# HGRN heads: the next head's projections in ten portions between the tile steps, operands of two heads side by side, diagonal blocks placed by one product

## The chip, the core and the metric

The kernel runs on one core of a Trainium2 chip. The core has five engines with queues of their own: TensorE (PE; its weight loads are shown apart as PEld), VectorE (DVE), ScalarE (ACT), GpSimd (POOL) and SyncE (SP, which issues DMAs). Each works through its queue in order; they wait for one another through semaphores. The metric is the device time of one execution in microseconds; lower is better.

## What is computed

Two transformer blocks of 256 tokens, one after the other, in float32. The change touches one mixer of the second block, HGRN2: four heads with key and value width 128, over 256 latent and 256 context tokens, forwards and backwards, with a decay per key column:

```python
def forget_gate(f_raw, lb):
    z = f_raw.astype(jnp.float32)
    log_f = jnp.logaddexp(jnp.log(lb), jnp.log1p(-lb) + jax.nn.log_sigmoid(z))
    k = (1.0 - lb) * jax.nn.sigmoid(-z)
    return k, log_f

def step(S, inp):                       # one chunk of 32 tokens
    qc, kc, gc, vc = inp
    b = jnp.cumsum(gc, axis=2)
    diff = b[:, :, :, None, :] - b[:, :, None, :, :]
    decay = jnp.exp(jnp.where(tri, diff, -jnp.inf))
    scores = jnp.einsum("bhtd,bhtsd,bhsd->bhts", qc, decay, kc)
    o = jnp.einsum("bhts,bhsv->bhtv", scores, vc) + jnp.einsum("bhtd,bhdv->bhtv", qc * jnp.exp(b), S)
    ...

def readout(o, g):
    return (rms_norm(o, out_norm_w).reshape(B_, n, B_V_W) * jax.nn.silu(g)).astype(g.dtype)
```

Queries are `silu(h @ w)` times a scale; here `lb` is zero, so the key is `sigmoid(-z)` and the log decay is `log_sigmoid(z)`. Each head needs five projections of the same 512 token columns: queries (Q), forward and backward forget logits (K0, K1), values (V) and gates (G), each by a 1024 x 128 weight.

## The kernel before

`hgrn_phase` (L2249) holds one program per engine. Matrix products of float32 are made from three products of rounded parts: a weight is split into `w_hi` (a rounding copy, ACT, L2485) and `w_lo` (the rest, by subtraction); the tokens `h_hi`, `h_lo` lie ready. So one projection is 8 x 3 = 24 matmuls of 512 columns (`part`, L2354), and values with gates together are 4 x 24 matmuls of 256 columns (`values_and_gates`, L2363).

A head's attention goes over eight tile steps, two directions by four tiles of 128 tokens. In step u TensorE makes the sums of the log decays over nine ranges (`sums`, L2389, six matmuls into banks 0 to 2), ACT takes their exponential into `e` (L2534, double buffered), VectorE multiplies seven of them with the queries into `qd` (L2671) and one into `qs` (L2673), GpSimd does the same with the keys, `kd` and `ke` (L2611, L2613). TensorE makes the scores of five short ranges and the diagonal in 32 x 32 blocks, and of two long ranges in end blocks (`scores`, L2405, L2408, L2411, banks 3 and 4). VectorE masks the blocks (`pm`, L2656) and adds the six up, once for each quarter of the partitions, right into the diagonal of the probabilities `pr` (L2662); ACT copies the end blocks beside them (L2526). TensorE multiplies `pr` with the values into bank 7 (L2418), one step later. After the eight tiles come the products between tiles (`cross_scores` L2437 into banks 5 and 6, `px` L2545, `cross_values` L2444), the norm of the output (ACT L2551 and L2554, VectorE L2689 and L2693) and its transposes (L2451), copied to `y_T` (L2575).

The next head's five projections run after the tile steps of this one, between those last products: `part(i+1, 0)` after step 8, 1 and 2 about the cross scores, values and gates last, into banks 0 to 4, which the tile steps use also. `w_hi` and `w_lo` have two slots; GpSimd subtracts for parts 0 and 1 (L2601), VectorE for 2 to 4 (L2625). ACT takes the queries' silu and the keys' sigmoid straight from PSUM (L2489, L2494), keeps `|z|` (L2495), and makes the log decay by exp and ln (L2500, L2503) and VectorE's L2642; TensorE turns it to token-major (L2373), ACT and VectorE split it (L2515, L2631). All five weights of a head are loaded by SP in one go when the split of the former head is done. The first three heads run in a hardware loop (`heads`, with `eng.Fori`), the fourth is written out.

The order on each engine is written out by hand: what stands first in the text goes first.

## Time and profile before

| | us |
|---|---|
| median of 3 runs | 2715.73 (2714.08 to 2720.18) |
| the profiled execution, device time | 2714.51 |
| its span, first to last instruction | 2712.7 |
| PE busy | 2422.6 (89%) |
| PEld busy | 2084.3 (77%) |
| DVE busy | 1358.3 (50%) |
| ACT busy | 1135.7 (42%) |
| POOL busy | 212.1 (8%) |
| mean granted TensorE clock | 0.923 of full speed |

The rows come from the profiled execution. Busy time is the time in which an engine's instructions run; matmuls are pipelined, so a busy PE can still be below its peak. The granted clock is the share of 2.4 GHz that TensorE was given (1.0 is 2.4 GHz, 0.5 is 1.2 GHz; numbers between are a mixture over a stretch). An idle time ends with a releaser: who gave the last semaphore, or "issue" where nothing in the profile shows what was waited for. The HGRN phase is some 13% of the span; all else is the same code before and after.

### The profile page before, as it was taken

To read this page: it belongs to the slowest core of one execution; us is meant where nothing else is said; L and a number is where in the kernel's file an instruction comes from. 1 tells how busy PE (TensorE), PEld (TensorE's weight loads), DVE (VectorE), ACT (ScalarE), POOL (GpSimd) and SP (SyncE) were. 2 spreads that over 40 slices of the span, in tenths; PEclk is the share of its full clock that TensorE was granted. 3 is DMA by queue.
4 is the path that set the end of the run, shared out by engine and by line. 5 is a ranking of instruction groups with operands and counts; after the bars stand their busy time and mean duration, and the time that the engine had idled before them with its cause. 6 is when DMAs were issued, how large, how long until landed. Compare 5 with 4: busy or idle time off the path is not lost. (4 is left out here: it accounts for less than half of the span.)

```text
span 2712.7 us, 42379 instructions
## 1 busy us (share of the span) xinstructions
PE 2422.6 (89%) x16488; PEld 2084.3 (77%) x16488; DVE 1358.3 (50%) x2193; ACT 1135.7 (42%) x1993; POOL 212.1 (8%) x185
## 2 busy tenths in 40 slices
PE   7998999998998998998768887678999989996998
PEld 6887978887887977887446776566888778875997
DVE  5443246445444236444445556646555554435665
ACT  3443254334434234443264444334333444444554
POOL 1000001001000001000003324300000000001000
PEclk9999899998999979999897888788999987997999
DMA  7876124875786323885121120023333362202663
GB/s 226 258 244 187 34 67 138 249 249 154 239 246 207 69 63 93 240 254 158 51 61 40 40 70 0 1 62 109 115 116 115 103 171 63 71 32 88 199 186 93
DMA packets 395134, 350.09 MB, mean 129 GB/s; under 512 B 25364, under 2 KB 358408, under 8 KB 394504
## 3 DMA queue, kind: packets, MB, share of 16 engines
q1 hardware_dynamic: 384932, 297.81, 38.1%
q10 hardware_dynamic: 10084, 50.66, 5.2%
q8 instruction: 81, 1.33, 0.2%
q14 instruction: 37, 0.30, 0.0%
HBM read 347.38 MB, written 1.05 MB: 128 GB/s over the span
## 5 line engine op out<-in xcount | busy, mean ns | idle before, releaser
L523 PE MATMUL ps<-x_hi,gu_hi 128*128 128x256 f32 x1680 | 478.4, 285 | 0.0
L523 PE MATMUL ps<-x_lo,gu_hi 128*128 128x256 f32 x1680 | 475.4, 283 | 0.0
L523 PE MATMUL ps<-x_hi,gu_lo 128*128 128x256 f32 x1680 | 475.4, 283 | 0.0
L523 PEld LDWEIGHTS ps<-x_hi,gu_hi 128*128 128x128 f32 x1680 | 321.9, 192 | 22.6 <-DVE gu_lo L668 17.5
L523 PEld LDWEIGHTS ps<-x_lo,gu_hi 128*128 128x128 f32 x1680 | 322.2, 192 | 2.6
L523 PEld LDWEIGHTS ps<-x_hi,gu_lo 128*128 128x128 f32 x1680 | 322.2, 192 | 0.0
L668 DVE TENSOR_TENSOR gu_lo<-w_gu,gu_hi 128x1024 fp32r<-128x1024 f32 x220 | 266.9, 1249 | 87.0 <-ACT gu_hi L599 87.0
L599 ACT ACTIVATE gu_hi<-w_gu 128x1024 fp32r<-128x1024 f32 x220 | 221.9, 1051 | 44.9 <-issue 30.0
L610 ACT ACTIVATE silu<-ps 128x256 f32<-128x256 f32 x88 | 33.8, 384 | 418.7 <-PE ps L523 404.8
L694 DVE SCALAR_TENSOR_TENSOR hid<-silu,ps 128x256 f32<-128x256 f32 x88 | 37.0, 421 | 316.9 <-ACT silu L610 316.8
L549 PE MATMUL ps<-dn_hi,h_hi 128*128 128x512 f32 x440 | 173.9, 395 | 6.4 <-DVE h_lo L703 6.3
L549 PE MATMUL ps<-dn_lo,h_hi 128*128 128x512 f32 x440 | 173.1, 393 | 0.0
L549 PE MATMUL ps<-dn_hi,h_lo 128*128 128x512 f32 x440 | 171.7, 390 | 0.0
L676 DVE TENSOR_TENSOR dn_lo<-w_dn,dn_hi 128x1024 fp32r<-128x1024 f32 x110 | 133.8, 1220 | 10.7 <-ACT dn_hi L603 10.7
L819 PE MATMUL ps<-both_x_hi,gu_hi 128*128 128x512 f32 x336 | 130.7, 389 | 0.0
L819 PE MATMUL ps<-both_x_lo,gu_hi 128*128 128x512 f32 x336 | 130.7, 389 | 0.0
L819 PE MATMUL ps<-both_x_hi,gu_lo 128*128 128x512 f32 x336 | 130.7, 389 | 0.0
L603 ACT ACTIVATE dn_hi<-w_dn 128x1024 fp32r<-128x1024 f32 x110 | 115.1, 1051 | 17.3 <-PE ps L549 17.3
L549 PEld LDWEIGHTS ps<-dn_hi,h_hi 128*128 128x128 f32 x440 | 83.3, 189 | 22.0 <-issue 7.4
L977 DVE SCALAR_TENSOR_TENSOR conv<-ps,par,conv 128x510 f32<-128x510 f32 x44 | 30.9, 745 | 134.4 <-ACT conv L914 134.4
L549 PEld LDWEIGHTS ps<-dn_hi,h_lo 128*128 128x128 f32 x440 | 83.1, 189 | 18.2
L549 PEld LDWEIGHTS ps<-dn_lo,h_hi 128*128 128x128 f32 x440 | 83.4, 190 | 13.4
(419 smaller groups left out, 5354.0 us busy)
## 6 DMA issues: line engine op xcount, KB each, us to landing
w_gu<-in_ffn_w_up SPq DMA_DIRECT2D x178, 512.0 KB, 6.1
w_dn<-in_ffn_w_down SPq DMA_DIRECT2D x134, 512.0 KB, 3.7
w_mod<-in_w_mod ACTq DMA_DIRECT2D x64, 768.0 KB, 6.4
w_gu<-in_ffn_w_gate SPq DMA_DIRECT2D x90, 512.0 KB, 5.1
odd_w<-in_odd_w_qkv SPq DMA_DIRECT2D x24, 512.0 KB, 5.2
w_gu<-in_ffn_w_down SPq DMA_DIRECT2D x11, 1024.0 KB, 4.9
hgrn_w<-in_even_w_in SPq DMA_DIRECT2D x20, 512.0 KB, 7.0
w_in_q<-in_w_in SPq DMA_DIRECT2D x2, 3072.0 KB, 10.9
```

The lines of the kernel that those rows point to most:

```text
L523: last = pe.matmul(gu(n)[:, a, :], wt[n][:, a, f, :], x[:, f, :], start=(f == 0 and p == 0), stop=(f == FT - 1 and p == 2), skip_group_che ...
L549: last = pe.matmul(k.ps[:, 2 * tt + c, :], h[n][:, tt * P:(tt + 1) * P], wt[n][:, c * BANK:(c + 1) * BANK], start=(first and p == 0), stop ...
L599: act.activation(gu_hi[n][:, a, :, :], wgu[n][:, a, :, :], ACT.Copy).then_inc(s["w_hi"], 1)
L603: act.activation(dn_hi[n][:, :], wdn[n][:, :], ACT.Copy).then_inc(s["w_hi"], 1)
L610: act.activation(sil[n][:, :], gu(n)[:, 0, :], ACT.Silu).then_inc(s["act_done"], 1)
L668: last = dve.tensor_tensor(gu_lo[n][:, a, :, :], wgu[n][:, a, :, :], gu_hi[n][:, a, :, :].bitcast(F32), ALU.subtract)
L676: dve.tensor_tensor(dn_lo[n][:, :], wdn[n][:, :], dn_hi[n][:, :].bitcast(F32), ALU.subtract).then_inc(s["dn_split"], 1)
L694: dve.scalar_tensor_tensor(hid[n][:, :], sil[n][:, :], 0.5, gu(n)[:, 1, :], ALU.mult, ALU.mult).then_inc(s["h_full"], 1)
L819: last = pe.matmul(gu(n, a), wt[n][:, a, f, :], x[:, f, :], start=(f == 0 and p == 0), stop=(f == FT - 1 and p == 2))
L977: dve.scalar_tensor_tensor(cv[n][:, a, :, 1:S], streams(n, a)[:, :, 0:S - 1], conv.tap(0, t, a), cv[n][:, a, :, 1:S], ALU.mult, ALU.add).t ...
```

## The change

Everything in it lies in `hgrn_buffers`, `hgrn_load` (one raw weight, in the order K0, K1, Q, G, V) and `hgrn_phase`, with one more constant (`c_blk`, ones in the four 32 x 32 blocks of the diagonal).

- The projections of head i+1 are cut into ten portions (`slot`): two each for K0, K1, Q, and four token tiles of gates and values. Portion u stands in tile step u, between sums and scores; portions 9 and 10 stand behind the last step. From the second head on all go into bank 6, one projection after the other, and ACT copies each out as it is (`keep_keys`, `keep_queries`, `keep_values`). For the first head there are five banks.
- `q`, `kk` and `vg` (values and gates) have two halves, one for each of two heads in turn. The silus come later, from SBUF, together (`silus`); the key is now exp(-softplus(z)), with VectorE's `max(z,0)+ln(...)` ahead of ACT's exp, so that no sigmoid is used.
- Raw weights come one projection at a time through two slots (`w_in`), the split weights through three; all `w_lo` are made by VectorE.
- `kd` and `ke` move from GpSimd to VectorE. VectorE adds up all 128 partitions at once into a narrow `prc`; GpSimd spreads it over the four diagonal blocks with one product with `blk` (`place`), which also writes the zeros around them, and takes the column `tot` (`total`).
- End blocks have two banks (4, 5), and the cross scores use banks 4 and 5 now. `px` has one buffer; the cross products of the two directions follow each other. The value product of a tile comes three steps later, the norm and the output of a head in the next head's first steps.
- The head loop is written out for all four heads on every engine.

```diff
+WRING = 3
+RAWRING = 2
+HGRN_PARTS = (1, 2, 0, 4, 3)
...
+    K0, K1, Q, G, V = range(5)
+    VG01, VG23 = 3, 4
+    SLOTS = [(K0, 0), (K0, 1), (K1, 0), (K1, 1), (Q, 0), (Q, 1), (VG01, 0), (VG01, 1), (VG23, 0), (VG23, 1)]
+    LAST = BH - 1
...
+            END_PS = [k.ps[:, 4 + n, 0:3 * SUB] for n in range(2)]
+            X_PS = flat[:, 4 * BANK:4 * BANK + 6 * P]
...
+            def proj_bank(h, c):
+                return k.ps[:, (4, 5, 6, 3, 7)[c] if h == 0 else 6, :]
...
+                for p in range(RAWRING, 5 * BH):
+                    sp.wait_ge(s["w_lo"], p - RAWRING + 1)
+                    dst, src = hgrn_load(m, w, p)
+                    sp.dma_start(dst, src).then_inc(w_in[p % RAWRING], 16)
...
+                def slot(h, n):
+                    c, half = SLOTS[n]
+                    bank = proj_bank(h, c)
+                    pe.wait_ge(s["w_lo"], 5 * h + (c if c < VG01 else V) + 1)
+                    if half == 0 and h:
+                        pe.wait_ge(s["proj_used"], 5 * h + c)
+                    if c < VG01:
+                        for f in range(4 * half, 4 * half + 4):
+                            for p, (wt, x) in enumerate(SPLITS):
+                                last = pe.matmul(bank, wt[:, f, (5 * h + c) % WRING, :], x[:, f, :], start=(f == 0 and p == 0),
+                                                 stop=(f == FT - 1 and p == 2))
                     else:
+                        tt = 2 * (c - VG01) + half
                         for f in range(FT):
                             for p, (wt, x) in enumerate(SPLITS):
+                                last = pe.matmul(bank[:, half * 2 * P:(half + 1) * 2 * P].rearrange("p (a n) -> p a n", a=2),
+                                                 x[:, f, tt * P:(tt + 1) * P], wt[:, f, gate_and_value(h)[2], :],
+                                                 start=(f == 0 and p == 0), stop=(f == FT - 1 and p == 2), skip_group_check=True)
+                    if half == 1:
+                        last.then_inc(s["proj_done"], 1)
...
+                    if d == 0:
+                        pe.wait_ge(s["ends_ready"], unit(i, NU - 1))
...
+                for n in range(8):
+                    slot(0, n)
+                turn_decays(0)
+                for n in range(8, 10):
+                    slot(0, n)
+                sums(0, 0)
+                for i in range(BH):
+                    more = i < LAST
+                    for u in range(NU):
+                        if u:
+                            sums(i, u)
+                        if more:
+                            slot(i + 1, u)
+                        if u == 2 and i:
+                            turn_out(i - 1)
+                        if u >= 1:
+                            scores(i, u - 1)
+                        if u >= 3:
+                            values(i, u - 3)
+                    if more:
+                        turn_decays(i + 1)
+                        slot(i + 1, 8)
+                    scores(i, NU - 1)
+                    values(i, NU - 3)
                     cross_scores(i, 0)
                     if more:
+                        slot(i + 1, 9)
+                    values(i, NU - 2)
+                    cross_values(i, 0)
                     cross_scores(i, 1)
+                    values(i, NU - 1)
                     if more:
+                        sums(i + 1, 0)
+                    cross_values(i, 1)
+                turn_out(LAST)
...
+                def split(h, j):
+                    p = 5 * h + j
+                    if p >= RAWRING:
+                        act.wait_ge(w_in[p % RAWRING], 16 * (p // RAWRING))
+                    if p >= WRING:
+                        before = p - WRING
+                        act.wait_ge(s["proj_done"], before // 5 * 5 + (before % 5 if before % 5 < G else VG23) + 1)
+                    act.activation(w_hi[:, :, p % WRING, :], wh[:, p % RAWRING, :, :], ACT.Copy).then_inc(s["w_hi"], 1)
...
+                def keep_keys(h, d):
+                    act.wait_ge(s["proj_done"], 5 * h + d + 1)
+                    if h:
+                        act.wait_ge(s["g_turned"], 2 * h)
+                    act.activation(ab[:, d, :], proj_bank(h, d), ACT.Abs).then_inc(s["abs_ready"], 1)
+                    act.activation(z[:, d, :], proj_bank(h, d), ACT.Copy).then_inc(s["proj_used"], 1)
...
+                def decay_tile(i, u):
+                    act.wait_ge(s["cum_done"], unit(i, u))
+                    n = i * NU + u - 2
+                    if n >= 0:
+                        act.wait_ge(s["side_done"], n + 1)
+                        act.wait_ge(s["tot_ready"], n + 1)
...
+                def score_ends(i, u):
+                    d = UNITS[u][0]
+                    act.wait_ge(s["sc_done"], unit(i, u))
+                    act.wait_ge(s["placed"], unit(i, u))
...
+                for i in range(BH):
+                    more = i < LAST
+                    for u in range(NU):
+                        decay_tile(i, u)
+                        if u >= 2:
+                            score_ends(i, u - 2)
+                        if u == 0:
+                            if more:
+                                split(i + 1, K1)
+                            if i:
+                                norm(i - 1)
+                        if u == 1 and more:
+                            keep_keys(i + 1, 0)
+                        if u == 2:
+                            if more:
+                                split(i + 1, Q)
+                            if i:
+                                keep_output(i - 1)
+                        if u == 3 and more:
+                            split(i + 1, G)
+                            keep_keys(i + 1, 1)
+                        if u == 4 and more:
+                            split(i + 1, V)
+                            soft_exp(i + 1)
+                        if u == 5 and more:
+                            keep_queries(i + 1)
+                        if u == 6 and more:
+                            soft_ln(i + 1)
+                        if u == 7 and more:
+                            keep_values(i + 1, VG01)
+                            keys(i + 1)
+                    if more:
+                        decays_hi(i + 1)
+                    score_ends(i, NU - 2)
+                    score_ends(i, NU - 1)
+                    keep_cross(i, 0)
+                    if more:
+                        keep_values(i + 1, VG23)
+                        silus(i + 1)
+                    keep_cross(i, 1)
+                    if i + 2 <= LAST:
+                        split(i + 2, K0)
...
+                def place(i, u):
+                    pool.wait_ge(s["p_ready"], unit(i, u))
+                    n = i * NU + u - 2
+                    if n >= 0:
+                        pool.wait_ge(s["pv_done"], n + 1)
+                    pool.tensor_tensor(pr[:, u % 2, :].rearrange("p (b n) -> p b n", n=SUB), m.blk[:, :].rearrange("p (b n) -> p b n", n=SUB),
+                                       prc[:, u % 2, :].unsqueeze(1).broadcast_to([P, P // SUB, SUB]), ALU.mult).then_inc(s["placed"], 1)
...
+                def decays(h):
+                    for d in range(2):
+                        dve.wait_ge(s["ln_step"], 2 * h + d + 1)
+                        dve.wait_ge(s["proj_used"], 5 * h + d + 1)
+                        dve.scalar_tensor_tensor(keys_of(h, d), z[:, d, :], 0.0, ab[:, d, :], ALU.max, ALU.add).then_inc(s["k_pre"], 1)
+                        dve.scalar_tensor_tensor(z[:, d, :], z[:, d, :], 0.0, ab[:, d, :], ALU.min, ALU.subtract).then_inc(s["g_ready"], 1)
...
+                def products(i, u):
+                    d, tt = UNITS[u]
+                    if u == 0:
+                        dve.wait_ge(s["k_ready"], 2 * i + 2)
+                        dve.wait_ge(s["q_ready"], i + 1)
+                        if i:
+                            dve.wait_ge(s["x_done"], 2 * i)
+                    dve.wait_ge(s["e_ready"], unit(i, u))
+                    n = i * NU + u - 2
+                    if n >= 0:
+                        dve.wait_ge(s["sc_done"], n + 1)
+                    key, qry = kk[:, i % 2, d, tt, :], q[:, i % 2, tt, :]
+                    times = lambda to, a, n, b: dve.tensor_tensor(to, a, b.unsqueeze(1).broadcast_to([P, n, P]), ALU.mult)
+                    times(kd[:, u % 2, :, :], e[:, u % 2, 1:N8, :], NLV, key)
+                    times(qd[:, u % 2, :, :], e[:, u % 2, 1:N8, :], NLV, qry).then_inc(s["qk_ready"], 1)
+                    dve.tensor_tensor(ke[:, u, :], e[:, u % 2, 0, :], key, ALU.mult)
+                    dve.tensor_tensor(qs[:, u, :], e[:, u % 2, N8, :], qry, ALU.mult).then_inc(s["side_done"], 1)
...
+                def probs(i, u):
+                    dve.wait_ge(s["sc_done"], unit(i, u))
+                    if u >= 2:
+                        dve.wait_ge(s["p_ready"], unit(i, u - 2))
+                    dve.tensor_tensor(pm[:, u % 2, :], SC_PS, lvl[:, UNITS[u][0], :], ALU.mult).then_inc(s["masked"], 1)
+                    dve.wait_ge(s["masked"], unit(i, u))
+                    if u >= 2:
+                        dve.wait_ge(s["placed"], unit(i, u - 2))
+                    dve.reduce_sum(prc[:, u % 2, :], pm[:, u % 2, :].rearrange("p (n t) -> p t n", t=SUB), AX.X).then_inc(s["p_ready"], 1)
...
+                for i in range(BH):
+                    more = i < LAST
+                    for u in range(NU):
+                        products(i, u)
+                        if u >= 1:
+                            probs(i, u - 1)
+                        if u == 0 and more:
+                            split(i + 1, K1)
+                        if u == 1 and i:
+                            norm(i - 1)
+                        if u == 2 and more:
+                            split(i + 1, Q)
+                        if u == 3 and more:
+                            split(i + 1, G)
+                        if u == 4 and more:
+                            split(i + 1, V)
+                        if u == 6 and more:
+                            decays(i + 1)
                     cross_operands(i)
                     if more:
+                        decays_lo(i + 1)
+                    probs(i, NU - 1)
                     if more:
+                        queries_and_gates(i + 1)
+                    if i + 2 <= LAST:
+                        split(i + 2, K0)
+                norm(LAST)
```

The order on VectorE in one tile step with a weight split in it. Before (`hgrn_tot` is the total decay, `pm` the masked scores):

```order
L2670 COPY hgrn_tot<-hgrn_e 128x1
L2671 TENSOR_TENSOR hgrn_qd<-hgrn_e,hgrn_q 128x896
L2673 TENSOR_TENSOR hgrn_qs<-hgrn_e,hgrn_q 128x128
L2656 TENSOR_TENSOR hgrn_pm<-ps,hgrn_lvl 128x192
L2662 TENSOR_REDUCE hgrn_p<-hgrn_pm 32x32 x4
```

and now:

```order
L2744 TENSOR_TENSOR hgrn_kd<-hgrn_e,hgrn_k 128x896
L2744 TENSOR_TENSOR hgrn_qd<-hgrn_e,hgrn_q 128x896
L2747 TENSOR_TENSOR hgrn_ke<-hgrn_e,hgrn_k 128x128
L2748 TENSOR_TENSOR hgrn_qs<-hgrn_e,hgrn_q 128x128
L2754 TENSOR_TENSOR hgrn_pm<-ps,hgrn_lvl 128x192
L2758 TENSOR_REDUCE hgrn_pc<-hgrn_pm 128x32
L2708 TENSOR_TENSOR hgrn_w_lo<-hgrn_w,hgrn_w_hi 128x8x128
```

The keys' products have come to VectorE, the column copy has gone, one reduction stands where four stood, and a `w_lo` follows in five of eight steps.

TensorE in one tile step, sums, scores, value product. Before:

```order
L2389 MATMUL ps<-hgrn_cum,hgrn_g_hi 128x384
L2389 MATMUL ps<-hgrn_cum,hgrn_g_lo 128x384
...
L2405 MATMUL ps<-hgrn_qd,hgrn_kd 32x32 x20
L2405 MATMUL ps<-hgrn_q,hgrn_k 32x32 x4
L2408 MATMUL ps<-hgrn_qd,hgrn_kd 32x32 x2
L2411 MATMUL ps<-hgrn_qd,hgrn_kd 64x64
L2418 MATMUL ps<-hgrn_v,hgrn_p 128x128
```

and now:

```order
L2427 MATMUL ps<-hgrn_cum,hgrn_g_hi 128x384
L2427 MATMUL ps<-hgrn_cum,hgrn_g_lo 128x384
...
L2396 MATMUL ps<-hgrn_h_hi,hgrn_w_hi 128x512
L2396 MATMUL ps<-hgrn_h_lo,hgrn_w_hi 128x512
L2396 MATMUL ps<-hgrn_h_hi,hgrn_w_lo 128x512
...
L2446 MATMUL ps<-hgrn_qd,hgrn_kd 32x32 x20
L2446 MATMUL ps<-hgrn_q,hgrn_k 32x32 x4
L2449 MATMUL ps<-hgrn_qd,hgrn_kd 32x32 x2
L2452 MATMUL ps<-hgrn_qd,hgrn_kd 64x64
L2463 MATMUL ps<-hgrn_vg,hgrn_p 128x128
```

A portion of twelve matmuls with the next head's weights stands between the sums and the scores of the tile before.

TensorE behind the eighth step of a head, now: scores of tile 7, a value product, cross scores of direction 0, portion 10, a value product, cross values, then direction 1. `px` is the copy of the cross scores.

```order
L2446 MATMUL ps<-hgrn_qd,hgrn_kd 32x32 x20
L2446 MATMUL ps<-hgrn_q,hgrn_k 32x32 x4
L2449 MATMUL ps<-hgrn_qd,hgrn_kd 32x32 x2
L2452 MATMUL ps<-hgrn_qd,hgrn_kd 64x64
L2463 MATMUL ps<-hgrn_vg,hgrn_p 128x128
L2471 MATMUL ps<-hgrn_qs,hgrn_ke 128x128 x2
...
L2471 MATMUL ps<-hgrn_qx,hgrn_ke 128x128
L2402 MATMUL ps<-hgrn_w_hi,hgrn_h_hi 128x256
...
L2463 MATMUL ps<-hgrn_vg,hgrn_p 128x128
L2477 MATMUL ps<-hgrn_vg,hgrn_px 128x128 x6
L2471 MATMUL ps<-hgrn_qs,hgrn_ke 128x128 x2
```

Of the projections only these 24 small matmuls of portion 10 and portion 9 ahead of the scores are left between the heads; before, three parts of 24 matmuls and the 96 of values and gates stood there.

## Rows read from the trace of the kernel before

**Rows 1.** stretches: length, busy us (instructions) of PE, PEld, DVE, ACT, POOL, clock, DMA.

```profile
1461.00:1502.00 41.00, 27.81 (x493) 22.59 (x493) 37.62 (x60) 15.85 (x34) 29.38 (x18) 0.68 0.01 2
1502.00:1543.00 41.00, 39.47 (x239) 34.83 (x240) 11.85 (x23) 23.05 (x38) 2.20 (x1) 0.95 0.26 65
1510.00:1526.00 16.00, 16.00 (x96) 14.10 (x95) 3.00 (x4) 8.19 (x11) 0.00 (x0) 1.00 0.00 0
1705.00:1746.00 41.00, 26.98 (x496) 21.07 (x494) 37.56 (x63) 15.37 (x34) 26.09 (x16) 0.74 0.01 2
```

**Rows 2.** ACT timeline, start and head 1: start us, us, line, [idle before].

```profile
1420.87 2.00 ACT L2485 ACTIVATE hgrn_w_hi<-hgrn_w 128x1024 fp32r<-128x1024 f32 x2 [0.28 <-PEq L204]
...
1462.48 1.13 ACT L2534 ACTIVATE hgrn_e<-ps 128x1152 f32<-128x1152 f32 x1 [1.23 <-PE ps L2389]
```

**Rows 3.** ACT timeline, the fourth (last) head.

```profile
1707.54 1.13 ACT L2534 ACTIVATE hgrn_e<-ps 128x1152 f32<-128x1152 f32 x1 [0.96 <-PE ps L2389]
...
1738.17 1.13 ACT L2534 ACTIVATE hgrn_e<-ps 128x1152 f32<-128x1152 f32 x1 [1.70 <-PE ps L2389]
...
1763.13 0.60 ACT L2575 ACTIVATE y_T<-ps 128x512 f32<-128x512 f32 x1 [2.40 <-PE ps L2451]
```

**Rows 4.** a stretch, L2354 (K and Q projections) alone: PE, PEld, clock.

```profile
1511.60:1516.60 5.00, 5.00 (x24) 4.13 (x22) 1.00 0.00 0
```

**Rows 5.** the same of L2363 (gates and values).

```profile
1450.00:1456.00 6.00, 6.00 (x52) 6.00 (x52) 1.00 1.13 270
```

**Rows 6.** stretches, PE alone: a value product and six sums; one scores.

```profile
1736.50:1738.00 1.50, 1.42 (x8) 1.00 0.00 0
1739.30:1740.50 1.20, 0.94 (x54) 1.00 0.05 14
```

**Rows 7.** stretches of L2437 (cross scores), L2444 (cross values), L2373 (transposes), each alone.

```profile
1509.90:1511.70 1.80, 1.50 (x12) 1.42 (x12) 1.00 0.00 0
...
1523.50:1526.60 3.10, 2.84 (x24) 2.73 (x24) 1.00 0.00 0
...
1539.20:1540.40 1.20, 1.04 (x8) 0.81 (x8) 1.00 0.00 0
```

**Rows 8.** timeline of the first tile step, VectorE beside GpSimd.

```profile
1463.69 2.08 POOL L2611 TENSOR_TENSOR hgrn_kd<-hgrn_e,hgrn_k 128x896 f32<-128x896 f32 x1 [37.01 <-ACT hgrn_e L2534]
1463.71 3.00 DVE L2671 TENSOR_TENSOR hgrn_qd<-hgrn_e,hgrn_q 128x896 f32<-128x896 f32 x1
```

**Rows 9.** instructions on tile hgrn_e: ns min/median/max, first, last start.

```profile
L2534 ACT ACTIVATE hgrn_e<-ps x32: 1131/1131/1132, 1462.5 to 1738.2; 128x1152 f32<-128x1152 f32 x32
...
L2671 DVE TENSOR_TENSOR hgrn_qd<-hgrn_e,hgrn_q x32: 1081/2218/3226, 1463.7 to 1741.3; 128x896 f32<-128x896 f32 x32
L2613 POOL TENSOR_TENSOR hgrn_ke<-hgrn_e,hgrn_k x32: 450/1302/1415, 1465.7 to 1741.4; 128x128 f32<-128x128 f32 x32
L2673 DVE TENSOR_TENSOR hgrn_qs<-hgrn_e,hgrn_q x32: 279/540/2423, 1466.6 to 1742.3; 128x128 f32<-128x128 f32 x32
```

**Rows 10.** groups by form, the phase: xcount, busy us, mean ns, idle.

```profile
L2662 DVE TENSOR_REDUCE hgrn_p<-hgrn_pm 32x32 f32<-32x192 f32 x128 | 61.7, 482 | 2.4
...
L2625 DVE TENSOR_TENSOR hgrn_w_lo<-hgrn_w,hgrn_w_hi 128x1024 fp32r<-128x1024 f32 x12 | 14.7, 1226 | 44.9 <-ACT hgrn_w_hi L2485 44.9
...
L2656 DVE TENSOR_TENSOR hgrn_pm<-ps,hgrn_lvl 128x192 f32<-128x192 f32 x32 | 11.1, 347 | 0.1
...
L2642 DVE SCALAR_TENSOR_TENSOR hgrn_abs<-ps,hgrn_abs 128x512 f32<-128x512 f32 x8 | 5.2, 692 | 13.7 <-ACT hgrn_abs L2503 13.7
...
L2503 ACT ACT_TABLE_LOAD x4 | 5.1, 1283 | 0.1
```

**Rows 11.** tile hgrn_w: loads, issue to landing.

```profile
DMA to landing us min/median/max: 3.8/7.0/10.3
```

**Rows 12.** waits, looped head 2, then unlooped head 4: us, times, longest.

```profile
PEld ps L2405 <- issue: 1.4, 3, 0.5
...
PEld ps L2405 <- issue: 3.6, 3, 2.2
```

461 lines of the change are left out of this document (173 added, 288 removed).

## The prediction, made before the changed kernel was run

> **What bounds the kernel now.** The granted-clock view came first (one core, mean 0.923), then busy time by stretch. The change touches one phase, the HGRN heads, from 1420.9 to 1763.7 us [rows 2, 3]: 342.8 us. Everything else keeps its instructions. The first exponentials of heads 1 and 4 start at 1462.48 and 1707.54 [rows 2, 3], so one head lasts 245.06 / 3 = 81.7 us. It has two halves. In the tile loop (41 us) VectorE is busy 37.6 us, GpSimd 29.4, TensorE 27.8 at a granted clock of 0.68; in the transition (41 us) TensorE is busy 39.5 at 0.95 and VectorE 11.9, GpSimd 2.2 [rows 1]. Each half is bound by one side while the other rests. That is the point to see: the sum of both engines' work is far below the sum of the halves.
>
> Why is VectorE full in the loop? `qd` starts at 1463.71 and takes 3.00 us; `kd` on GpSimd starts 0.02 earlier and takes 2.08; the fastest `qd` takes 1.08 [rows 8, 9]. 2.08 + about 1.0 is 3.0: one engine stands still while the other multiplies. The small products show it too: `ke` 0.45 at best and 1.30 in the median, `qs` 0.28 and 0.54 [rows 9]. The Trainium skill ("SBUF — State Buffer", Who interferes with whom) says that VectorE and GpSimd share a port pair under an exclusive lock, held for a whole instruction; the trace agrees (3.00 for 2.08 plus 1.0).
>
> **The change, part by part.** *Removed from VectorE's path:* waiting for GpSimd's 2.08 us product, and three of four reductions of 0.48 us per tile [rows 8, 10]. *Added:* `kd` and `ke`. A tile step now costs VectorE 2 x 1.08 + 2 x 0.28 + 0.35 + 0.48 = 3.55 us [rows 9, 10]; I take the one 128-partition reduction at the 0.48 of the 32-partition one, because both read 192 elements per partition (bounds: 0.48, and 1.93 for four). GpSimd keeps a one-column copy and one 128x128 product: 0.45 us, or 1.30 with VectorE in its way [rows 9]. That takes up to 0.45 from VectorE. Per head VectorE has 8 x 4.0 = 32, five `w_lo` of 1.23 (two were GpSimd's) = 6.1, four decay steps of 0.69 = 2.8 (two before) [rows 10], and some 6 unchanged: 47 us.
>
> *Moved:* TensorE's projections of the next head. At clock 1.00, 24 matmuls of 512 columns fill 5.00 us and 52 of 256 columns 6.00 [rows 4, 5]: a K or Q portion (12) is 2.5 us, a gate-and-value portion (24) 2.8. One head then is: K0, K1, Q 72 x 0.21 = 15.1; gates and values 96 x 0.115 = 11.0; sums with a value product 8 x 1.42 = 11.4; scores 8 x 0.94 = 7.5 [rows 6]; cross scores 2 x 1.50 = 3.0, cross values 2.8, decay transposes 1.0 [rows 7], output transposes (four of the same) 0.5, the zeroing product about 1.0 (an estimate, two 512-column passes at twice 0.21, rounded up). Sum 53.3. With no gap in the queue the clock should stay up: it was 1.00 in the stretch in which TensorE was busy 16 of 16 us and 0.95 with 39.5 of 41 [rows 1]; I take 0.95, so 56.1.
>
> *New waits.* (1) `cross_scores(0)` now waits for `ends_ready` of tile 7, since its banks 4 and 5 hold the end blocks. Queued on VectorE before it: tile 7's scores end 1.0 after portion 9; mask and reduction 0.9, placing 0.5, ACT's three end copies 0.7; TensorE has one value product of 0.3 meanwhile: 2.1 idle. Behind that wait stand portion 10 and both cross values. (2) At the first step of a head ACT has table load, exponential, a split of 1.05, the previous head's four squares (1.2), table load, root, table load, then the second exponential: 1.28 + 1.13 + 1.05 + 1.2 + 1.28 + 0.3 + 1.28 + 1.13 = 8.7 us [rows 9, 10], while TensorE has cross values 1.4, portion 1, sums, portion 2 and scores, 8.5; sums(2) follow ACT. About 1 us idle. (3) The single projection bank 6: portion 3 waits for ACT to copy K0 out (two copies, 1.1 us); TensorE has scores and sums, 2.1 us, in between. Cost nothing, unless ACT is late. (4) The raw weights come through a ring of two. A load takes 3.8 to 10.3 us [rows 11]; each is wanted two portions or more (10 us) after its slot is free. Nothing; SP's queue holds nothing else but the four output-row loads, which go out in head 3. (5) For small hand-overs I add 2 us a head. 56.1 + 2.1 + 1 + 2 = 61.2: **61 us a head**. In a step TensorE has 5.0 us, VectorE 4.0, or 5.2 with a `w_lo`: near each other, which is why the high end is wide. ACT has some 41 us a head, with six table loads of 1.28.
>
> On those table loads the Trainium skill ("ScalarE: Activation LUTs", What ACT_TABLE_LOAD costs) adds a drain of 1.38 us to each load of 1.28. The trace disagrees: the loads of L2503 stand 1283 ns, 0.1 us idle in front of four of them together [rows 10].
>
> *Start.* `w_lo` of the first part moves from GpSimd to VectorE, the projections run in the order K0, K1, Q, G, V with values last. Q's load can only start when K0's split is done, about 1423.3, lands by 1434 at the worst and is wanted at 1436. TensorE then is through at about 1455, but ACT still copies the last bank, does two silus behind a table load and reloads: first exponential about 1459, 3 us earlier. One us of it is given back in the next head, whose offset is smaller: net 2. *Last head.* No portions to hide; VectorE at 4.0 a tile against (1738.17 - 1707.54) / 7 = 4.38 now [rows 3], but with the previous head's norm inside it: nothing to 3 us. Its tail has cross values and cross scores in turn through one `px` buffer (+1) and one reduction instead of four, twice (-3). Together 2.
>
> **Sum.** 3 x (81.7 - 61) + 2 + 2 = 66 us. The profiled execution took 2714.5 (span 2712.7), 1.2 below the median of 2715.7; 2714.5 - 66 = 2648.5, **2648 us**.
>
> Bounds: at clock 1.00 and with waits of 2.7 only, a head is 56: -81, 2633. If VectorE and the lock set the pace at 6.0 a step, and the transition keeps 22: 70 a head, -39 + 3 for a last head that gains nothing: 2682.
>
> **Rivals.**
> 1. *Partly late ACT or VectorE.* The portions fit, but each step waits about 1.2 us for bank 6 to be copied out or for VectorE behind `w_lo`: 61 + 10 = 71 a head; 2714.5 - 32 - 2 = 2680. For it: 5.2 against 5.0 us in five steps; in-order ACT. Against: averages of 47 and 41 in 61.
> 2. *The clock stays down.* Loops of scores ran at 0.68 and 0.74 [rows 1]. If the mixed stream is granted 0.72, 53.3 becomes 74, with 3 idle 77: 2714.5 - 14 - 2 = 2698. Against: TensorE had a third of that stretch idle, and will not.
> 3. *Slower: the chain closes.* If in each step the next sums wait for everything before them (portion 2.8, sums 1.1, exponential 1.3, products 2.7, scores 0.9, mask and reduction 0.9, placing 0.5 to 1.3, ends 0.7), a step is 11 us and a head 88 + 22 = 110: 2714.5 + 85 = 2800. It decides from a step of (81.7 - 22) / 8 = 7.5 us on. Against: buffers of e, kd, qd, pm and pr are double, end blocks now too, and the value product comes three steps late, so only sums to exponential to sums (2.4) and portion to copy to portion are tight.
> 4. *Unlooped code.* All heads are now straight code. In looped head 2 issue waits before scores are 1.4 us in total, in the straight head 4 3.6, longest 2.2 [rows 12]. At twice 2.2 a head more: 65, 2661. The Trainium skill ("Runtime: NRT & Kernel Launch", Instruction fetch mechanics) says that taken branches stall the fetch and straight code streams; by that rule this rival costs nothing.
> 5. *Table drain.* Were the drain there, three loads near the head's edge would add 4 us a head: 2714.5 - 54 = 2661. The skill's page above gives that rule; the row speaks against it.
> 6. *Nothing gained*: the phase is reordered and late waits eat all. 2714.5.
>
> **Chances.** Forecast 0.68 (own range 2633 to 2664), rival 1 0.14, 2 0.05, 3 0.05, 4 0.03, 5 0.01, 6 0.04. Leaving out 2, 3, 6 and a little of the rest, the range is 2630 to 2685. A measurement tells about 0.2% (5.4 us) from no change: faster 0.91, same 0.03, slower 0.06.
>
> **What would show it.** First exponentials of heads 61 us apart; TensorE busy over 90% and granted 0.95 or more between them; `kd` and `qd` 1.1 us each; the placing product 0.5 to 1.3; one idle gap of about 2 us a head before cross scores. Wrong if the sums wait on ACT in most steps, if the portions wait for bank 6, or if the granted clock in the loop stays near 0.7.

## The result and the profile after

| | before | after |
|---|---|---|
| median, us | 2714.9 (4 runs, 2712.4 to 2720.2) | 2630.7 (4 runs, 2627.9 to 2632.6) |
| ratio, 95% interval | | 0.9687 [0.9668, 0.9705] |
| profiled execution, us | 2714.5 | 2632.3 |
| its span | 2712.7 | 2630.5 |
| mean granted clock | 0.923 | 0.937 |
| PE busy in the span | 2422.6 | 2389.3 |

The kernel became 84 us faster; the forecast was 66. The two profiled executions differ by 82.2, and 81.8 of it lie in the phase: it ends at 1681.9 in place of 1763.7 [rows 3]. ScalarE's timeline after, first exponential of each head and the last copy (it answers [rows 2, 3]):

```profile
1458.75 1.13 ACT L2585 ACTIVATE hgrn_e<-ps 128x1152 f32<-128x1152 f32 x1
...
1515.42 1.13 ACT L2585 ACTIVATE hgrn_e<-ps 128x1152 f32<-128x1152 f32 x1
...
1572.94 1.13 ACT L2585 ACTIVATE hgrn_e<-ps 128x1152 f32<-128x1152 f32 x1
...
1629.53 1.13 ACT L2585 ACTIVATE hgrn_e<-ps 128x1152 f32<-128x1152 f32 x1
...
1681.29 0.60 ACT L2611 ACTIVATE y_T<-ps 128x512 f32<-128x512 f32 x1 [2.37 <-PE ps L2484]
```

The first exponential stands 3.7 us earlier. Three heads take 56.9 us each in place of 81.7, which makes 74.3. The last head with its tail takes 52.4 in place of 56.2, which makes 3.8. Together that is 81.8.

Stretches of after, one head each (columns as [rows 1]); then the tile steps and the edge of the second head apart:

```profile
1458.70:1515.40 56.70, 53.07 (x710) 47.07 (x710) 38.13 (x65) 34.60 (x61) 13.68 (x16) 0.97 0.13 39
1515.40:1572.90 57.50, 55.01 (x726) 48.28 (x726) 39.45 (x70) 38.69 (x73) 12.95 (x16) 1.00 0.16 47
1572.90:1629.50 56.60, 54.59 (x724) 48.03 (x725) 38.21 (x69) 37.78 (x72) 12.95 (x16) 1.00 0.20 67
1629.50:1682.00 52.50, 32.58 (x552) 26.49 (x551) 30.19 (x62) 23.10 (x58) 12.48 (x16) 0.82 0.01 1
...
1515.40:1557.00 41.60, 41.48 (x571) 35.34 (x572) 34.30 (x61) 30.67 (x59) 12.20 (x15) 1.00 0.22 65
1557.00:1573.00 16.00, 13.59 (x158) 13.00 (x157) 5.14 (x10) 8.10 (x16) 0.75 (x2) 1.00 0.00 1
```

The two halves of a head [rows 1] have become one. In the eight tile steps TensorE is busy 41.48 of 41.60 us at the full 2.4 GHz; all its idle time stands in the last 16 us. VectorE has 39 of 57, so TensorE bounds a head. Its waits from 1515 to 1573 us (us, times, longest):

```profile
PE ps L2471 <- ACT hgrn_p L2594: 1.9, 1, 1.9
PE ps L2396 <- DVE hgrn_w_lo L2708: 1.1, 2, 0.5
```

The first is `cross_scores(0)` behind ScalarE's end copies; the second is portion 1 behind a late `w_lo`, 0.5 us for each of the two head edges that touch the window. The first has a price beyond its length. In the first head the same wait of 1.9 us ends at 1503.5, and behind it TensorE falls to its low level (1.2 GHz) for some 3 us while it is fully busy; in the second and third head it does not fall:

```profile
1502.00:1504.00 2.00, 0.51 (x2) 0.54 (x3) 0.10 (x1) 0.60 (x3) 0.45 (x1) 0.78 0.00 0
1504.00:1506.00 2.00, 2.00 (x12) 2.00 (x11) 0.00 (x0) 0.00 (x0) 0.00 (x0) 0.50 0.03 8
1506.00:1508.00 2.00, 2.00 (x16) 2.00 (x16) 0.00 (x0) 0.81 (x1) 0.00 (x0) 0.87 0.00 0
```

That is the 0.97 of the first head. What VectorE and GpSimd do, by tile and by form (it answers [rows 9, 10]):

```profile
L2685 POOL COPY hgrn_tot<-hgrn_e x32: 183/1084/1213, 1459.9 to 1661.5; 128x1 f32<-128x1 f32 x32
L2744 DVE TENSOR_TENSOR hgrn_kd<-hgrn_e,hgrn_k x32: 1079/1092/1349, 1460.0 to 1660.1; 128x896 f32<-128x896 f32 x32
L2744 DVE TENSOR_TENSOR hgrn_qd<-hgrn_e,hgrn_q x32: 1077/1085/1353, 1461.0 to 1661.1; 128x896 f32<-128x896 f32 x32
...
L2758 DVE TENSOR_REDUCE hgrn_pc<-hgrn_pm 128x32 f32<-128x192 f32 x32 | 16.1, 503 | 1.1
...
L2693 POOL TENSOR_TENSOR hgrn_p<-hgrn_blk,hgrn_pc 128x128 f32<-128x128 f32 x32 | 25.9, 810 | 83.4 <-DVE hgrn_pc L2758 80.7 <-PE ps L2463 2.7
...
L2607 ACT ACT_TABLE_LOAD x4 | 5.1, 1283 | 0.1
```

`qd` fell from a median of 2218 ns to 1085. The exclusion between the two engines is still there, but now GpSimd pays: its one-column copy takes 183 ns at best and 1084 in the median, the length of one of VectorE's wide products.

### The profile page after: what moved, and what is told of

It reads as the page before. It is cut to its first block and busy times, and to the rows that moved or that the text cites. A ratio compares the mean times of both kernels' runs of the same rounds, so it can differ in the third digit from the quotient of the medians.

```text
span 2630.5 us, 42098 instructions
## 1 busy us (share of the span) xinstructions
PE 2389.3 (91%) x16488; PEld 2060.9 (78%) x16488; DVE 1317.9 (50%) x2144; ACT 1135.1 (43%) x1996; POOL 140.4 (5%) x177
```

## The experiments

Single executions of one kernel spread over up to 12 us, and the medians of the kernel before, measured anew beside each group of runs, lie between 2712.4 and 2714.9. So the length of the phase (ScalarE's first split to the start of its last `y_T` copy, from the timelines) stands beside the medians. It repeats better: 260.7 and 260.3 in two executions of the changed kernel. A ratio is to the kernel before that was measured beside the run. A head is the time from its first exponential to that of the next head.

| kernel | median us | ratio to before | phase us | heads 1, 2, 3 us |
|---|---|---|---|---|
| before | 2714.9 | | 342.3 | 81.0, 81.3, 82.8 |
| after | 2630.7 | 0.9687 | 260.7 | 56.7, 57.5, 56.6 |
| e1 portions behind | 2683.6 | 0.9883 | 310.2 | 70.7, 75.0, 74.1 |
| e2 keys on GpSimd | 2636.1 | 0.9711 | 262.2 | 56.1, 57.3, 57.9 |
| e3 two products | 2618.4 | 0.9651 | 246.8 | 51.2, 54.9, 51.5 |
| e4 VectorE loaded | 2641.1 | 0.9729 | 270.1 | 58.8, 60.5, 58.1 |
| e5 fill | 2629.0 | 0.9688 | 255.9 | 54.0, 56.3, 55.3 |
| e6 both | 2626.1 | 0.9675 | 253.2 | 53.1, 55.4, 55.4 |
| e7 four openings | 2624.3 | 0.9673 | 250.5 | 52.3, 54.6, 54.6 |
| e8 before, filled | 2722.2 | 1.0030 | 351.7 | 86.5, 89.0, 82.7 |
| e9 before, straight | 2712.7 | 1.0002 | 341.8 | 80.8, 82.9, 80.8 |
| e10 filled, straight | 2714.4 | 0.9999 | 340.8 | 81.5, 81.7, 81.8 |
| e11 before, keys moved | 2713.2 | 1.0002 | 341.5 | 82.3, 82.1, 81.9 |
| e12 one opening | 2622.0 | 0.9675 | 250.6 | 52.3, 54.6, 54.6 |
| e13 portions only | 2640.0 | 0.9725 | 267.9 | 58.0, 59.3, 59.8 |
| e14 before, placing | 2777.0 | 1.0230 | 406.7 | 98.6, 98.8, 98.7 |
| e15 after again | 2630.6 | 0.9696 | 260.3 | 56.9, 57.6, 56.6 |
| e16 one opening again | 2621.4 | 0.9660 | 250.6 | 52.3, 54.6, 54.6 |
| e17 placing, ends late | 2726.3 | 1.0052 | 355.0 | 84.8, 85.5, 85.4 |

### Which part made the gain: e1, e13

```diff
e1, TensorE (ScalarE and VectorE likewise):
                     for u in range(NU):
-                        if more:
-                            slot(i + 1, u)
...
                     if more:
+                        for n in range(8):
+                            slot(i + 1, n)
                         turn_decays(i + 1)
```

> The changed kernel with portions 1 to 8 of the next head's projections, and the steps of ScalarE and VectorE that go with them, put behind the tile loop again instead of one into each tile step; the loop stays written out, the side-by-side operands, the one reduction and the product that places the blocks stay. Theory (the time was won because TensorE's product work, some 30 us a head, now fills the gaps of a loop that VectorE sets): the eight steps go back to VectorE's pace of about 3.9 us, some 32 us, and the stretch behind them takes some 42 us, so a head takes 74 us in place of 56.9; three heads make it 51 us slower than the changed kernel, about 2682 us, and the granted clock in the tile stretch falls below 0.9. Rival (the cheaper placing and the removal of the lock between VectorE and GpSimd made the gain, and the interleaving little): a head takes under 64 us, and the kernel comes out below 2652 us.

2683.6 (0.9883 [0.9866, 0.9899]), forecast 2682: 53 of the 84 us are lost with the interleaving (50 by the phase). A head has two halves again, here the second:

```profile
1528.90:1561.00 32.10, 20.71 (x441) 16.71 (x442) 25.62 (x47) 16.66 (x38) 11.81 (x14) 0.89 0.07 19
1561.00:1603.90 42.90, 37.19 (x287) 32.79 (x285) 14.04 (x24) 22.59 (x36) 2.36 (x3) 1.00 0.17 50
```

The stretch of 32 us against 41 [rows 1] is what a lighter VectorE, the freed lock, the second end bank and the later values gave together: 29 us over the kernel. e13 takes the first two of these four away and keeps the portions in the tile steps.

```diff
e13, VectorE (the keys' products are GpSimd's, as in e2; pr as before):
-                    dve.reduce_sum(prc[:, u % 2, :], pm[:, u % 2, :]....)
+                    for i4 in range(P // SUB):
+                        b4 = slice(i4 * SUB, (i4 + 1) * SUB)
+                        last = dve.reduce_sum(pr[b4, UNITS[u][0], u % 2, b4], pm[b4, u % 2, :]....)
```

> The changed kernel with both reliefs of VectorE taken back: the keys' two products are GpSimd's again, and the diagonal blocks are four reductions of VectorE straight into place, with no product that places them; the portions between the tile steps and the side-by-side operands stay. VectorE then has about 1.15 + 0.83 + 0.35 + 4 x 0.48 = 4.3 us a step and its part of the next head's work, 5.2 a step in the mean against the 5.1 to 5.7 that TensorE sets. Theory (the interleaving is the gain; once TensorE sets the step, VectorE's reliefs hide): 57.5 to 60 us a head, 2633 to 2645 us. Rival (both engines are near their limit, and the lock and the reductions come through): 63 us a head or more, 2655 us or more, with a clock below 0.95 in the tile stretch.

```profile
1514.30:1573.60 59.30, 55.41 (x727) 48.26 (x727) 49.90 (x78) 39.07 (x74) 28.42 (x24) 1.00 0.16 46
```

2640.0, inside the theory's range: 74 of the 84 us are there with both reliefs of VectorE taken back. VectorE is 10 us busier than after, and TensorE's clock is 1.00 in this head all the same (0.97 in the other two). Once TensorE sets the step, 10 us of VectorE's work a head are worth 2 (59.0 against 56.9).

Read the two runs with care: e13 keeps the second end bank, the later value products and the later norm, and so does e1. So 74 is the portions with these three, 29 is these three with VectorE's reliefs, and the sum of both exceeds 84 in part because the three are in both. What the runs do bound is each group as the last one added: the portions 53, the reliefs 9. No run has the portions without the second end bank and the later values; what those are worth beside the portions stays open.

### How far the next engines are: e2, e3, e4

```diff
e2, GpSimd:
+                    pool.tensor_tensor(kd[:, u % 2, :, :], e[:, u % 2, 1:N8, :], key...., ALU.mult).then_inc(s["qk_k"], 1)
+                    pool.tensor_tensor(ke[:, u, :], e[:, u % 2, 0, :], key, ALU.mult).then_inc(s["side_k"], 1)
e3, TensorE:
+                    parts = SPLITS if h == 0 else SPLITS[:2]
e4, VectorE:
+                    dve.reduce_sum(spare[:, :], e[:, u % 2, 1:N8, :], AX.X).then_inc(s["spare_done"], 1)
```

> The changed kernel with the two products of the keys (the wide one of 128x896 and the small one) handed back to GpSimd, which then makes them beside VectorE's products of the queries; all else stays. Theory of the lock (the two engines exclude each other while they read and write, as the wide product of the queries took 3.00 us beside GpSimd and 1.08 at best): one step then has VectorE and GpSimd in turn for about 1.1 + 2.1 + 0.5 + 0.35 + 0.6 of VectorE and the placing, 4.8 to 5.4 us, against the 5.1 of a step that TensorE sets now; so the step grows by 0.3 to 1.0 us, 2.4 to 8 us a head, and the kernel ends 8 to 25 us later, at 2639 to 2656 us, with gaps on TensorE and a clock below 1.00. Rival (with TensorE as the bound the lock no longer reaches the end): within 4 us of the changed kernel, 2627 to 2635 us.

```profile
L2756 DVE TENSOR_TENSOR hgrn_qd<-hgrn_e,hgrn_q 128x896 f32<-128x896 f32 x8 | 9.2, 1152 | 5.7 <-ACT hgrn_e L2586 5.7
...
L2696 POOL TENSOR_TENSOR hgrn_kd<-hgrn_e,hgrn_k 128x896 f32<-128x896 f32 x8 | 18.9, 2368 | 0.0
```

The lock falls the other way here: GpSimd begins a step with its one-column copy, VectorE gets in first, and `qd` takes 1152 ns while `kd` takes 2368. The kernel before shows the same twice, in the first two steps of its last head: where `qd` starts first, it takes 1.08 and 1.28 us and `kd` 3.02 and 2.93; in the other steps `kd` starts first. The heads stay at 57.1 in the mean against 56.9. The median of 2636.1 lies between the two forecasts (2627 to 2635 and 2639 to 2656). Median and phase are 5 and 1.5 us above after, and the intervals ([0.9694, 0.9727] and [0.9668, 0.9705]) overlap: the rival holds for the heads, a small loss is not excluded. e2 has both engines under the lock and loses next to nothing; whether the order or TensorE as the bound makes it harmless, it does not separate.

> The changed kernel with the third of the three products of each portion (low part of the weights with high part of the activations) left out for heads 2 to 4, so their projections are less exact and the output is not the reference's; the low parts are still made. That takes 8 x 8 = 24 instructions of 512 columns (24 x 0.21 = 5.0 us) and 32 of 256 columns (32 x 0.115 = 3.7 us) a head off TensorE, 8.7 us. Theory (TensorE sets the head): a head goes from 56.9 to 48 to 51 us, until the chain exponential, products, scores, mask, reduction, placing or VectorE's 39.5 us shows; three heads make 18 to 26 us, about 2605 to 2613 us. Rival (the chain through the exponentials sets the 5.1 us of a step, and TensorE merely looks busy since the products run as they are released): under 6 us in all, 2624 us or more. A second one: the gaps lower the granted clock from 1.00 and return the gain in part; then it lands between the two and the stretch shows a clock under 0.97.

```profile
1508.50:1563.40 54.90, 48.58 (x670) 42.48 (x670) 39.40 (x70) 38.71 (x73) 13.30 (x16) 0.94 0.17 49
1563.40:1614.90 51.50, 45.63 (x668) 39.72 (x669) 38.20 (x69) 37.86 (x72) 13.29 (x16) 1.00 0.22 73
```

Three heads gave 13.2 us, 4.4 a head of the 8.7 taken away; the median 2618 misses the 2605 to 2613 of the theory and passes the limit of the rival. TensorE sets the head, but a chain stands 4 to 5 us behind it: its waits rise to 6 us of 51.5. The second rival shows as well. Two heads with the same products on TensorE took 54.9 at a clock of 0.94 and 51.5 at 1.00. Of these 3.4 us, 0.9 also stand between the same two heads of the changed kernel (57.5 and 56.6, both at 1.00), so the clock took about 2.5. It fell, here too, behind the wait before the cross scores, which has grown to 2.9 us.

> The changed kernel with one more instruction on VectorE in each tile step, a sum over 128x896 elements of the exponentials into a scratch tile that nothing reads, ahead of the two wide products; it will take 0.95 to 1.3 us. It stands on the chain from the exponential to the scores and loads VectorE by 8 to 10 us a head, from 39.5 to about 49 of 57. Theory (TensorE sets the head and scores are issued one step behind the sums, so VectorE has about 2 us a step to spare): the head grows by under 1.5 us, the kernel by 0 to 6 us, to 2630 to 2636 us. Rival (VectorE is a close second, with waits on every step): the head grows by the whole of the added time, 8 to 10 us, the kernel by 30 to 40 us.

The sum took 1.08 us, 8.65 a head. Three heads grew by 6.7 us in all (2.2 a head, a quarter), and the last one, which has no portions beside it, by 5.1. Theory said under 1.5 a head and 2630 to 2636 us, the rival 8 to 10 a head: nearer the theory, outside its range. Part of the growth is clock. The three heads were granted 0.94, 0.97 and 1.00, the changed kernel's 0.97, 1.00 and 1.00; the third head, at 1.00 in both, grew by 1.5.

### The last waits: e5, e6, e7, e12, e15, e16

```diff
e5, TensorE (ScalarE likewise):
-                    cross_scores(i, 0)
                     if more:
                         slot(i + 1, 9)
                     values(i, NU - 2)
+                    cross_scores(i, 0)
e6, ScalarE, added to e5 (VectorE likewise):
+                    if i + 2 <= LAST:
+                        split(i + 2, K0)
                     if more:
                         ...
                         silus(i + 1)
e7 and e12, TensorE, added to e6:
-                        pe.matmul(k.ps[:, O, :], k.zero[:, :], k.x_T[:, 0, :], start=True, ...)
-                    pe.matmul(..., values_of(i, tt), start=False, stop=False, ...)
+                    pe.matmul(..., values_of(i, tt), start=(d == 0), stop=False, ...)      e7
+                    pe.matmul(..., values_of(i, tt), start=(u == 0), stop=False, ...)      e12
```

> The changed kernel with portion 10 moved ahead of the first cross product on TensorE (it stood behind it), and ScalarE's copy of its result ahead of the copy of the cross scores. TensorE waits 1.9 us a head there for ScalarE's copies of the last tile's ends (the one wait of over 0.6 us that is left in a head). Theory (TensorE sets the head, so what fills its one wait comes off the time): 1.3 to 1.9 us a head over three heads, 4 to 6 us, 2625 to 2627 us. Rival (the chain of the last tile, ends, cross scores, copy, cross values and the next exponential, sets the end of the head, not TensorE): no change, 2629 to 2632 us, or up to 2 us a head later.

> The same, and the split of the first weights of the head after next (the high part on ScalarE, the low part on VectorE) put ahead of the silus and of the scaling of queries and gates. TensorE waited 0.5 us a head for that low part, and the first exponential of a head stood about 1 us behind its sums. Theory: another 0.5 to 1 us a head, so 6 to 8 us under the changed kernel in all, 2622 to 2625 us. Rival: the silus come later instead, VectorE's scaled queries with them, and the first products of the head wait for them: no more than the run before gives, or 1 us a head worse than that.

> The run before, and without the product with zeros over 512 columns that opens the bank of the outputs once a head (1.1 us in the trace): the first four products of values, which each write 128 columns of their own, open their columns themselves. Theory (TensorE sets the head): 0.9 to 1.1 us a head, 3 to 4 us under the run before. Rival: it stood in a wait and is worth nothing. Third: opening 128 columns spoils what the neighbours hold, and the output is wrong; then the time still tells what the product costs.

> The version with portion 10 and the early split moved, without the product with zeros; only the first product of values of a head opens the bank, the other three tiles' first products add to it. Opening 128 columns per tile (the run before of this kind) gave a wrong output. Theory (an opening marks the whole bank, each place of which is then overwritten by the first product that reaches it): the output is right again, and the time is that of the wrong one, 2622 to 2626 us, 0.9 to 1.1 us a head under the version with the zeros. Rival (an opening marks the columns it writes): the three other tiles add to what the last head left, and the output is wrong.

The phase went from 260.7 to 255.9, 253.2 and 250.5 or 250.6, each step about as the theories have it (4.8, 2.7, 2.6). The medians say less: e5 (2629.0) lies in the range of its rival and is not told from after, e6 (2626.1) lies above its theory (2622 to 2625), e7 is 1.8 us under e6 where 3 to 4 were expected, and e12 (2622.0) is at the low end of its range. The 1.9 us wait is gone from TensorE; what stays is 0.7 a head before the cross values. That makes 1.2 and 1.3 us in the second and third head. The first gave 2.7, since its clock is 1.00 now and no longer 0.97: its busy time fell from 53.07 to 51.61 with the same work. e7 lost part of the outputs' sums (relative difference 0.085): an opening of the second tile's 128 columns made the first tile's next addition an overwrite. With one opening (e12) nothing is lost, though three tiles' first products then only add. So an opening reaches the whole bank. Side by side on one chip, the last two:

> The changed kernel once more, beside the next run on the same chip: 2627 to 2633 us.

> The version with portion 10 ahead of the first cross product, the early split and one opening of the outputs' bank, once more beside the changed kernel. By the traces a head is 54.6 us in place of 57.0. Theory: 6 to 9 us under the changed kernel on the same chip. Rival: the difference of the medians so far, 2622 against 2631, is one of chips and runs, and under 3 us is left.

```profile
1509.20:1563.70 54.50, 53.82 (x725) 47.82 (x725) 39.44 (x70) 39.03 (x72) 12.84 (x16) 1.00 0.17 50
```

2630.6 (2629.7 to 2633.5) against 2621.4 (2616.3 to 2627.2), 9.2 us (6 to 9 expected), and TensorE busy 53.8 of 54.5 us in a head. This version beats both kernels.

### Clock and loop: e8, e9, e10

```diff
e8, TensorE, tile loop of the kernel before:
                             sums(u)
+                            for f in range(FT):
+                                pe.matmul(k.ps[:, 6, :], h_hi[:, f, 0:P], h_hi[:, f, :], start=(f == 0), stop=(f == FT - 1), ...)
e9 and e10 (e10 on top of e8):
-                with eng.Fori(0, BH - 1) as i:
+                for i in range(BH - 1):
```

> The kernel before with eight added products of 512 columns (1.7 us at full clock) on TensorE in each of its tile steps, behind the sums; they write a bank that is idle then and nothing reads them. TensorE is busy 28.5 of 41.5 us in that stretch, at a mean granted clock of 0.66. Theory (VectorE and its lock with GpSimd set the 4 us step; the clock comes from TensorE's waits): the clock of the tile stretch rises to 0.9 or more, a head stays within 1.5 us of 81.7, the kernel within 6 us of 2713. Rival A (the low clock was itself what made the step slow, since scores at half speed stand in the chain): the head gets faster by 2 to 5 us, 2693 to 2705 us. Rival B (TensorE had no room): 1.7 us x 8 a head slower, 30 to 50 us, 2745 us or more, the clock staying below 0.8.

> The kernel before with its loop over the heads written out; nothing else. Theory (the loop costs next to nothing: at its turn TensorE shows an issue wait of 0.4 us): within 3 us of 2713. Rival (the issue waits come from code that is supplied more slowly, and written-out code is supplied worse): 4 to 12 us a head slower, 2725 us or more. Other rival (the turn of the loop costs what the trace of the filled kernel showed, 4 us a head): 2700 to 2707 us.

> The kernel before with the eight added products of 512 columns in each tile step and the loop written out. With the loop, the added products raised the granted clock of the tile stretch from 0.66 to 0.93 and shortened its seven steps from 4.64 to 4.20 us each, but the kernel became 7.5 us slower: a head took 86.5 to 89 us, with issue waits on TensorE of 4.0 us at the turn of the loop and of 5.8 us behind the last steps. Theory (these two waits come from the loop's longer code, not from the work): without the loop they go, a head takes 81.7 - 3.1 + 0.5 = 79 us or less, 2700 to 2708 us. Rival (they come from the number of instructions that TensorE's queue has to take in, in a loop or not): 2718 us or more.

From a head's first to its eighth exponential, before, e8 and e10 (stretches):

```profile
1462.50:1495.00 32.50, 23.30 (x384) 19.05 (x388) 30.78 (x49) 13.49 (x28) 23.57 (x14) 0.65 0.01 2
```

```profile
1460.90:1490.30 29.40, 28.03 (x433) 23.09 (x432) 27.75 (x45) 13.48 (x27) 21.48 (x14) 1.00 0.01 2
```

```profile
1465.00:1494.10 29.10, 27.96 (x433) 23.02 (x432) 27.38 (x45) 13.47 (x27) 21.49 (x13) 1.00 0.01 2
```

With work in TensorE's gaps the same loop was granted 1.00 and its exponentials came 3 us earlier. Yet in e10 the heads took 81.7 us, as before: the rest of the head grew from 48.5 to 52.3 us. The expected 79 did not come, and the kernel stayed at 2714, between the theory (2700 to 2708) and its rival (2718 or more). The trace of e10 shows a large part of what took the 3 us back, GpSimd and VectorE at the eighth step:

```profile
1497.96 5.48 POOL L2603 TENSOR_TENSOR hgrn_w_lo<-hgrn_w,hgrn_w_hi 128x1024 fp32r<-128x1024 f32 x2
1498.00 3.24 DVE L2673 TENSOR_TENSOR hgrn_qd<-hgrn_e,hgrn_q 128x896 f32<-128x896 f32 x1
1501.17 2.42 DVE L2675 TENSOR_TENSOR hgrn_qs<-hgrn_e,hgrn_q 128x128 f32<-128x128 f32 x1
```

GpSimd comes to the next head's two `w_lo` while VectorE still has the products of the last tile to make, and under the lock these take 5.7 us in place of the 3.3 of the kernel before, where `w_lo` starts as they end. So VectorE is through with the last operands of the head 44.2 us after its first exponential, in the kernel before 42.8. All three heads of e10 show this. It also meets the kernel before in one head of three: its third has steps of 4.27 us in place of 4.6 and a clock of 0.83 in place of 0.65 and 0.72, loses the time again behind `w_lo` (3.23 and 2.42 us) and takes 82.8 us, the longest of the three. In e9 it is the second head (4.33 us, 3.24 and 2.42, 82.9). A faster tile loop alone moves waits, not the end.

e8 was slower than e10 by 8 to 11 us, in its looped heads only, and its time lies in none of the three forecasts, though the clock rose as the theory has it. TensorE's timeline at the first turn of the loop, before and e8:

```profile
1540.64 0.67 PE L2378 MATMUL ps<-x_T,zero 128*128 128x512 f32 x1 [0.38 <-issue]
```

```profile
1543.30 1.19 PE L2378 MATMUL ps<-x_T,zero 128*128 128x512 f32 x1 [4.02 <-issue]
```

4.0 us without anything to wait for, 5.2 at the second turn, and in e10 no such gap at all. The two turns of the longer body cost 9.3 us, the shorter one's nothing that e9 could show (1.0002 [0.9993, 1.0011]). The 5.8 us issue wait behind the last steps stayed in e10; it is a wait for VectorE's mask that the weight queue has no name for.

### The VectorE parts alone: e11, e14, e17

```diff
e14, VectorE:
-                        for i4 in range(P // SUB):
-                            ...
+                        dve.reduce_sum(prc[:, u % 2, :], pm[:, u % 2, :]....).then_inc(s["p_ready"], 1)
e14, ScalarE, ahead of the end copies:
+                        act.wait_ge(s["placed"], i * NU + (u + 1))
e17, added to e14 (and end blocks in two banks):
-                        if u >= 1:
-                            score_ends(u - 1)
+                        if u >= 2:
+                            score_ends(u - 2)
```

> The kernel before with the two products of the keys taken from GpSimd and made on VectorE, as the changed kernel does; the rest stays, four reductions to a step and the loop among it. VectorE then has 1.08 + 1.08 + 0.28 + 0.28 + 0.35 + the four reductions (1.9 in all) + 0.1 = 5.1 us a step, against steps of 4.64 us before. Theory (VectorE's sum sets the step, the lock is gone): 0.4 to 0.5 us a step slower, 8 steps of four heads, 10 to 16 us, 2723 to 2729 us. Rival (the lock costs more than the shift: the wide product took 3.00 us): 0 to 10 us faster.

> The kernel before with one reduction over 128 partitions in place of the four, and GpSimd's product that places the blocks behind its keys' products of the next tile; nothing else. VectorE is 1.4 us a step lighter. Theory (VectorE set the tile steps of 4.64 us): steps of 3.9 to 4.2 us, 3 to 5 us a head, 2694 to 2702 us. Rival (the placing stands behind 2.4 to 3 us of the keys' products in GpSimd's queue, ScalarE's copies of the ends wait for it and the next exponential stands behind them): no change or slower, 2710 to 2725 us.

e11: 1.0002 [0.9993, 1.0011], neither theory's sign. Its tile steps did grow, to 5.00 us from 4.64, 4.59 and 4.27, as the theory has it; the rest of the head became shorter by nearly as much, 47.1 us in the mean against 50.2, and VectorE's last products there stand beside no `w_lo` of GpSimd any more. e14 came out 63 us slower, five times the worst that its rival allowed. One step of it, ScalarE, GpSimd and VectorE:

```profile
1482.36 1.11 ACT L2536 ACTIVATE hgrn_e<-ps 128x1152 f32<-128x1152 f32 x1
...
1483.58 3.00 DVE L2680 TENSOR_TENSOR hgrn_qd<-hgrn_e,hgrn_q 128x896 f32<-128x896 f32 x1
...
1486.50 0.54 DVE L2682 TENSOR_TENSOR hgrn_qs<-hgrn_e,hgrn_q 128x128 f32<-128x128 f32 x1
1486.96 0.34 DVE L2668 TENSOR_TENSOR hgrn_pm<-ps,hgrn_lvl 128x192 f32<-128x192 f32 x1
1487.34 0.47 DVE L2672 TENSOR_REDUCE hgrn_pc<-hgrn_pm 128x32 f32<-128x192 f32 x1
1487.90 0.45 POOL L2610 TENSOR_TENSOR hgrn_p<-hgrn_blk,hgrn_pc 128x128 f32<-128x128 f32 x1 [1.00 <-DVE hgrn_pc L2672]
1488.44 0.61 ACT L2528 ACTIVATE hgrn_p<-ps 32x32 f32<-32x32 f32 x3 [4.97 <-POOL hgrn_p L2610]
1488.96 1.11 ACT L2536 ACTIVATE hgrn_e<-ps 128x1152 f32<-128x1152 f32 x1
```

Read it as a ring of 6.60 us: the next exponential stands in ScalarE's queue behind the end copies, these wait for the placing, that for the reduction, and that stands on VectorE behind the products of the exponential. Before the placing existed, the end copies waited for the scores and for the value product of two tiles before, not for VectorE.

> The kernel before with the one reduction and the placing on GpSimd (which alone took 2777 us, with tile steps of 6.60 us), and the end blocks in two banks, so that ScalarE copies the ends of a tile one step later, behind the exponential of the tile after next, as the changed kernel does. Theory (the 6.60 us step is the ring exponential 1.13, products 3.0, small product 0.54, mask 0.34, reduction 0.48, placing 0.45, ends 0.61, exponential, in which only the place of the end copies is new): the ring is open, steps fall to 4.1 to 4.7 us, and a head to 78 to 82 us, 2700 to 2716 us. Rival (GpSimd's queue is the cause: the placing stands behind the keys' products, and the keys' products behind the placing): steps stay over 5.5 us and the kernel over 2740 us.

With the ring opened, steps are 4.73 us in the first head (33.1 for seven) and 4.85 to 4.88 in the next two, and the kernel takes 2726 (1.0052 [1.0033, 1.0072]), between the theory (2700 to 2716) and the rival (over 2740). So the ring was 51 of the 63 us. It is not all: 12 to 14 us stay and make the placing a loss on the kernel before. Their place is GpSimd's queue. The next head's first `w_lo` now stands behind the last placing and starts 41.1 us after the first exponential of its head in place of 37.0, and TensorE's first projection of the next head waits for it. TensorE's waits for GpSimd's `w_lo` from the first exponential on (us, times, longest), before and e17:

```profile
PE ps L2354 <- POOL hgrn_w_lo L2601: 0.7, 2, 0.4
```

```profile
PE ps L2357 <- POOL hgrn_w_lo L2605: 11.4, 3, 3.8
```

The later `w_lo` also meets VectorE's cross operands under the lock: in the first head `kx` takes 1327 ns and `qx` 1452 in the mean, against 284 and 281 before. These are readings of the trace; no run moved the `w_lo` ahead of the placing.

## Where the prediction was right and wrong

The direction, the place and the mechanism were right: three heads with TensorE as the bound. The size was not: the sum for one head was 4.3 us too long. The median of 2630.7 lies at the low end of the range (2630) and outside the forecast's own range (2633 to 2664). The missing 16 us are 3 x 4.1 in the heads, 1.7 at the start and 1.8 at the end. The sum for one head, term by term:

| term | forecast | measured |
|---|---|---|
| TensorE's work at full clock | 53.3 | 54.6 to 55.0 |
| clock 0.95 in place of 1.00 | 2.8 | 0 in heads 2 and 3; 1.5 in head 1 (0.97) |
| wait of `cross_scores(0)` for the end copies | 2.1 | 1.9 |
| first step of a head, ScalarE | 1 | 0 in heads 2 and 3; in head 1 another wait, 1.8 |
| bank 6, weights | 0 | 0; 0.5 for a late `w_lo` |
| small hand-overs | 2 | none in the trace |
| head | 61.2 | 56.9 |

The prediction's own low bound (clock 1.00, waits of 2.7: 56 a head, 2633 us) describes what came. Its high bound was mis-added: 2714.5 - 39 + 3 is 2678.5, not 2682. And by its own terms the wait before the cross scores is 0.9 + 0.5 + 0.7 less the value product of 0.3, which is 1.8; the 2.1 did not take the 0.3 off.

**The step that failed first is the clock.** The 0.95 was read from the mean of the transition [rows 1], as if it were what TensorE is granted at 96% busy. Cut finer, the same 41 us of the kernel before say something else:

```profile
1502.00:1504.00 2.00, 2.00 (x5) 1.61 (x6) 1.92 (x5) 1.50 (x2) 2.00 (x1) 0.50 0.00 0
1504.00:1506.00 2.00, 2.00 (x7) 1.52 (x6) 1.23 (x5) 0.00 (x0) 0.20 (x1) 0.50 0.03 8
1506.00:1508.00 2.00, 2.00 (x10) 1.60 (x9) 0.00 (x0) 0.00 (x0) 0.00 (x0) 0.90 0.00 0
...
1510.00:1543.00 33.00, 31.47 (x213) 28.37 (x212) 8.70 (x14) 21.33 (x36) 0.00 (x0) 1.00 0.32 80
```

The low level (1.2 GHz) of the tile loop lasted into the first 4 us of the transition, fully busy; the other 33 us, with 1.5 us of idle time in them, were at 1.00. The mean mixed an inheritance of the loop with the transition's own level. With no sparse loop ahead there is nothing to inherit, and 1.00 was the number to take, less what one wait can do (0.97 in the first head). The row of 16 busy us at 1.00, named in the same sentence, had said so.

**The second is the 2 us of hand-overs**, added without a row. In the tile steps TensorE is idle 0.12 us of 41.6: its queue always holds a portion that waits for nothing of that step, so no hand-over shows. The two errors, 4.8 us, outweigh the 1.3 us or more by which the work was put too low (the pieces were read from stretches of one kind of product; that each change of kind adds the tail of the last is a guess that no run tests).

**The third is the doubt on ScalarE's first step.** It took 6.0 us from the first exponential to the second in heads 2 and 3, with the table loads as forecast; but portion 1 and what follows gave TensorE work for that time. In head 1 no earlier head's norm stands there and the step takes 2.5 us. The 1.8 us of that head are TensorE's wait for the very first exponential, with no portion left to fill it.

*Right:* the wait of 2.1 before the cross scores, which e5 took away; bank 6 and the ring of weights at nothing (one wait of 4.5 us for a load, at the phase's start); the first exponential at 1459 (1458.75); the reduction over 128 partitions at 0.48 (503 ns, where 1.93 was the other bound); the placing at 0.45 to 1.3 (mean 0.81). The 1 us that the second head was to give back did not show: head 1 took no longer than the others. The last head gained 3.8 in place of 2: 1.4 in its seven steps (29.3 us against 30.6 [rows 3]), 2.4 in its tail. VectorE's sum of 47 a head came out as 43.3 by the durations of the second head's instructions: the 0.45 us a step that the lock was to cost it (3.6 a head) fell on GpSimd instead (`kd` 1.09 in the median against 1.08 at best). The 39 busy us of the stretch count overlapping ends once.

*Rivals.* Of partly late engines there is nothing in the steps, and e3 says how near it was: 4 to 5 us a head. The clock of 0.72 did not come: the tile steps were granted 1.00 with TensorE busy in all but 0.12 us of them; e3's head at 0.94 prices a smaller fall at about 2.5 us. The closing chain did not come either; the reason given against it fits, but no run tested it on the changed kernel. e14 shows the same kind of ring at full price in the kernel before, and e17 that the later end copies in a second bank are what opens it: the change's harmless-looking part. Unlooped code cost nothing (e9). The looped body of e8 lost 9.3 us at its two turns. There the Trainium skill ("Runtime: NRT & Kernel Launch", Instruction fetch mechanics) agrees in kind: it has a taken branch stall the fetch when its target is not in the pages at hand, and the 4.02 us at the turn against no gap in straight code would fit such a stall, though the short body of the kernel before shows only 0.38. No run shows the fetch itself. The drain that the Trainium skill ("ScalarE: Activation LUTs", What ACT_TABLE_LOAD costs) puts on a table load is again not there: four loads of 1283 ns have 0.1 us of idle time together.

## What to carry to other kernels

Where two halves of a loop are each bound by another engine, putting the work of one into the gaps of the other is worth most of what can be had (53 of 84 us here as the last part added; 74 with the second end bank and the later values). The reliefs that seem to be needed for it may hide behind it (9 us), and one of them alone can cost more than it gives when it puts a new link between an engine's queue and the next step. Read a granted clock in short stretches before it becomes a factor, since the mean of a busy stretch may carry the level of the idle one ahead of it. When the bound engine is busy 96%, look at what stands behind its one wait, and put there something that waits for nothing; the clock may give back more than the wait. And when a faster engine changes nothing, look at what the neighbour starts in the time that was won: here it was GpSimd's `w_lo`, under the lock that it shares with VectorE.

## What the runs showed of the hardware

- Starting an accumulation on 128 columns of a bank turned the next addition to other columns of the bank into an overwrite (e7 against e12). One start for the bank replaces a product with zeros over 512 columns (1.1 us, two instructions). The Trainium skill ("PSUM — Partial Sum Buffer", The four PSUM rules) states this rule, with a single start for the first product of a bank as one way to use it; both runs agree.
- The first turn of a loop showed TensorE idle for 0.38 us, and for 4.02 us with 64 more products in the body (e8; 5.24 at its second turn); straight code has neither.
- The three looped heads of the kernel before were granted 0.65, 0.72 and 0.83 over the same seven tile steps; with eight more products a step (e10) it was 1.00 in all three, and the heads still took 81.7 us in the mean.
- Behind one wait of 1.9 to 2.9 us TensorE's level fell to 1.2 GHz for some 3 to 5 us of full work (changed kernel, e3, e4); a wait of the same length in the changed kernel's second head was followed by 1.00. With the wait filled (e5, e6, e12) no head was below 1.00.
- Under the exclusion of VectorE and GpSimd the one that comes second pays what is left of the other's instruction: `qd` 3.00 us behind GpSimd's `kd` [rows 8], GpSimd's 0.18 us copy 1.08 behind VectorE's. The Trainium skill ("SBUF — State Buffer", Who interferes with whom) has it as a lock held for a whole instruction; both rows agree, and e2 shows the other order, with 1.15 us for VectorE's product and 2.37 for GpSimd's.
